# First stage of a hybrid block kernel: the order of the x, w_ada and w_in loads, and shift pieces summed on TensorE

## What is computed

```
sc = silu(c)
mod = sc @ w_ada + b_ada                       # w_ada: 1024 x 6144
sh1, sc1, ga1, sh2, sc2, ga2 = split(mod, 6)   # six chunks of 1024

h = rmsnorm(x, g_pre_mix) * (1.0 + sc1) + sh1
proj = h @ w_in                                # 1024 x 2560
uv = gelu(proj[..., :1024])                    # gMLP group
q, k, vv = split(proj[..., 1024:], 3)          # stick-breaking attention
...                                            # branches, w_out, residual with ga1
...                                            # second norm with sc2, sh2; router; 64 experts + shared; residual with ga2
```

## Time and profile before

| | us |
|---|---|
| runs shown: median | 1141.26 |
| lowest to highest of the 3 | 1138.83 to 1143.55 |
| the profiled execution | 1139.13 |
| its span, first to last instruction | 1137.4 |

### The profile page before, as it was taken

How to read it: one execution, slowest core, us unless ns; L and a number is a source line. 1 busy time by engine, 2 the same in 40 slices (tenths; PEclk the granted TensorE clock), 3 DMA queues, 4 the chain that set the end, 5 groups by cost and what they waited for, 6 DMA issues and landing times.

```text
span 1137.4 us, 14545 instructions
## 1 busy us (share of the span) xinstructions
PE 1042.1 (92%) x4500; PEld 725.2 (64%) x4500; DVE 761.9 (67%) x1282; ACT 568.2 (50%) x605; POOL 522.1 (46%) x222
## 2 busy tenths in 40 slices
PE   0699997979798999999999999999999999999975
PEld 0587775547663667766677667766677667666532
DVE  4649785652755677777777777777777777677247
ACT  4334135642341556655566556655566556655401
POOL 0233213540222466566655666566655666566300
PEclk9799998989998999999999999999999999999979
DMA  9756751202152599999999999999998889898296
GB/s 320 262 181 247 276 203 47 75 28 84 74 222 82 189 353 370 347 353 374 369 379 361 362 362 358 353 366 370 367 358 336 340 334 355 331 345 332 79 387 278
DMA packets 68903, 318.66 MB, mean 280 GB/s; under 512 B 18640, under 2 KB 19152, under 8 KB 41360
## 3 DMA queue, kind: packets, MB, share of 16 engines
q1 hardware_dynamic: 42096, 267.41, 61.4%
q0 software_dynamic: 23104, 47.50, 11.5%
q10 hardware_dynamic: 3680, 3.46, 1.0%
HBM read 317.25 MB, written 39.85 MB: 314 GB/s over the span
## 4 chain that ended last, share of the span: by engine, by line
PE 79%; DVE 9%; DMA 6%; issue 2%; ACT 2%; SPq 1%; ACTq 0%; DVEq 0%; POOLq 0%; POOL 0%
PE ps L1229 20%; PE ps L1210 11%; PE ps L1212 11%; PE ps L1211 11%; PE ps L942 8%; PE ps L993 7%; DMA yall<-y_rows 4%; PE ps L1143 2%; PE ps L1118 2%; DVE acc L1362 1%; DMA ada<-in_w_ada_dram 1%; PE ps L1049 1%; PE ps L1075 1%; PE ps L1163 1%; DMA hg<-h_rows,idxg 1%
## 5 line engine op out<-in xcount | busy, mean ns | idle before, releaser
L586 POOL DMA_INDIRECT hg<-h_rows,idxg x70 | 352.7, 5038 | 147.7 <-DVE idxg L1669 147.4
L1675 DVE TENSOR_TENSOR wlo<-raw,whi 128x2048 fp32r<-128x2048 f32 x134 | 300.6, 2285 | 0.0
L820 ACT ACTIVATE whi<-raw 128x2048 fp32r<-128x2048 f32 x136 | 261.4, 1923 | 0.1
L1229 PE MATMUL ps<-rawd,actt 128*128 128x512 f32 x544 | 244.5, 592 | 1.4 <-ACT actt L856 1.4
L1210 PE MATMUL ps<-whi,hthi 128*128 128x512 f32 x544 | 225.3, 414 | 0.0
L1212 PE MATMUL ps<-whi,htlo 128*128 128x512 f32 x544 | 213.0, 392 | 0.0
L1211 PE MATMUL ps<-wlo,hthi 128*128 128x512 f32 x544 | 212.8, 391 | 0.0
L1689 DVE TENSOR_TENSOR htlo<-ps,hthi 128x1024 fp32r<-128x1024 f32 x68 | 83.3, 1225 | 177.2 <-ACT hthi L852 177.2
L862 ACT ACTIVATE ysb<-ps 128x1024 f32<-128x1024 f32 x68 | 69.6, 1024 | 213.5 <-PE ps L1229 213.5
L1229 PEld LDWEIGHTS ps<-rawd,actt 128*128 128x128 f32 x544 | 102.8, 189 | 104.7 <-issue 97.8
L594 POOL DMA_INDIRECT y_rows<-ysb,idxs x68 | 73.2, 1076 | 161.1 <-ACT ysb L862 153.7
(11 more groups left out here) (247 smaller groups left out, 1283.0 us busy)
## 6 DMA issues: line engine op xcount, KB each, us to landing
raw<-in_w_gate_dram SPq DMA_DIRECT2D x68, 1024.0 KB, 7.6
raw<-in_w_up_dram SPq DMA_DIRECT2D x68, 1024.0 KB, 10.9
rawd<-in_w_down_dram SPq DMA_DIRECT2D x68, 1024.0 KB, 12.8
ada<-in_w_ada_dram SPq DMA_DIRECT2D x24, 1024.0 KB, 7.2
yall<-y_rows SPq DMA_DIRECT2D x8, 2048.0 KB, 24.3
wraw<-in_w_in_dram POOLq DMA_DIRECT2D x10, 1024.0 KB, 6.0
woraw<-in_w_out_dram SPq DMA_DIRECT2D x16, 256.0 KB, 2.7
xs<-in_x_dram SPq DMA_DIRECT2D x4, 512.0 KB, 10.8
```

The source lines that it names most:

```text
L586: gp.indirect_dma_start(out=hg[s][:, :, :].rearrange("p k q -> p (k q)"), out_offset=None, in_=h_rows, in_offset=bass.IndirectOffsetOnAxis ...
L820: A(whi[:, s, :, cols], raw[:, s, :, cols], ACT.Copy).then_inc(hi_ok, 1)
L1229: ins = mm(bank(4 + hf), actt[:, k, :], rawd[:, s, k, hf * 512:(hf + 1) * 512], start=(k == 0), stop=(k == KF - 1))
L1675: V.tensor_tensor(wlo[s][:, :, c0:c1], raw[:, s, :, c0:c1], whi[:, s, :, c0:c1].bitcast(F32), ALU.subtract).then_inc(lo_dve, 1)
```

## The change

Four things are moved, all in the first stage.

1. **SP's order.** x goes ahead of every piece of w_ada; then come the four SH1 pieces, the four SC1 pieces, then w_in pieces 0 and 1 (which POOL issued before), then GA1 and the rest. The ring `ada` has six buffers for the first eight pieces: pieces 0 to 5 go without a wait, 6 and 7 wait for `sh_mm` (PE is done with pieces 0 and 1). From piece 8 on there are two buffers.
2. **SH1 on PE.** For each SH1 piece PE runs four matmuls (two rows k, two halves of 512 columns) with sc_col[:, k] as the stationary operand (one column) and the piece as the moving one, adding up in banks 5 and 6, one partition. ACT copies the row of 1024 to `sh_row`, and eight matmuls with a strided set of 128 of its elements (one partition) as the stationary operand and a single one as the moving one bring it into columns. The transposes of z (k = 0 to 4) stand between the two, the others behind the scale's column sums.
3. **DVE** works out 1/rms first, then weighs only the four SC1 pieces.
4. **ACT and POOL.** `gb` and `bsp` are loaded by POOL instead of ACT and counted by `col_in`, for which DVE waits before a1c. `piece_high(0)` stands ahead of the wait for a1c and b1c, no longer behind k = 3.

The diff, cut to its core:

```diff
@@ sync @@
+            for t in range(TT):
+                sp.dma_start(xs[:, t, :], x[t * P:(t + 1) * P, :]).then_inc(x_in[t], 16)
...
+                if n == FIRST:
+                    load_win(0)
+                    load_win(1)
+                if ADA_SLOTS <= n < FIRST:
+                    sp.wait_ge(sh_mm, n - ADA_SLOTS + 1)
+                elif n >= FIRST:
+                    sp.wait_ge(ada_used, n - 5)
@@ gpsimd @@
+                gp.dma_start(gb[:, :], g_branch.rearrange("(k p) -> p k", p=P)).then_inc(col_in, 16)
+                gp.dma_start(bsp[:, :], b_spatial.rearrange("g i -> i g")).then_inc(col_in, 16)
@@ scalar @@
+            ac.wait_ge(sh_mm, 4)
+            A(sh_row[:, :], bank(5, 2)[0:1, :], ACT.Copy).then_inc(sh_ok, 1)
+            piece_high(0)
             ac.wait_ge(ab_ok, 1)
...
-                if k == KH - 1:
-                    piece_high(0)
@@ tensor @@
+            def shift_row(n):
...
+                pe.wait_ge(ada_in[ADA_SLOT[n]], 16 * ada_count(n))
+                for r in range(2):
+                    k = 2 * q + r
+                    for hf in range(2):
+                        ins = mm(bank(5 + hf)[0:1, :], sc_col[:, k:k + 1], ada[ADA_SLOT[n]][:, r, hf * 512:(hf + 1) * 512],
+                                 start=(k == 0), stop=(k == KD - 1))
+                ins.then_inc(sh_mm, 1)
@@ vector @@
+            factor(ST_X, D)
+            v.sem_inc(rs_x_ok, 1)
+            for n in range(FIRST // 2, FIRST):
                 weigh_piece(n)
...
+            v.wait_ge(vec_in, 16 * 4)
+            v.wait_ge(col_in, 16 * 2)
             v.wait_ge(mod_mm, 2)
```

More of the change, by code:

```diff
@@ L36 @@
 WO_RING = 3
+ADA_SLOTS = 6
 DG = 512
@@ L80, in block_kernel @@
         yall = at("yall", [P, TT, TOPK, D], F32, 0)
-        ada = [at("ada0", [P, 2, D], F32, 0), at("ada1", [P, 2, D], F32, 8 * KB),
-               at("ada2", [P, 2, D], F32, 136 * KB)]
+        ada = [at(f"ada{s}", [P, 2, D], F32, (0, 8, 136, 112, 120, 128)[s] * KB) for s in range(ADA_SLOTS)]
+        sh_row = at("sh_row", [1, D], F32, 188 * KB)
         acc = at("acc", [P, 2, D], F32, 16 * KB)
@@ L224, in block_kernel @@
         vec_in = sem("vec_in")
+        col_in = sem("col_in")
+        win_first = [sem(f"win_first{s}") for s in range(2)]
         row_in = sem("row_in")
         grow_in = sem("grow_in")
-        ada_in = [sem(f"ada_in{s}") for s in range(3)]
+        ada_in = [sem(f"ada_in{s}") for s in range(ADA_SLOTS)]
+        sh_mm = sem("sh_mm")
+        sh_ok = sem("sh_ok")
         ada_used = sem("ada_used")
@@ L348, in block_kernel, with ada_piece, ada_count @@
         SC1, SH1, GA1, SC2, SH2, GA2 = 1, 0, 2, 4, 3, 5
[L349 to L355, removed]
+        FIRST = 8
+        ADA_SLOT = [0, 1, 2, 3, 4, 5, 0, 1] + [n % 2 for n in range(FIRST, 24)]
+        def ada_piece(n):
+            return n // 4, n % 4
+        def ada_count(n):
+            return ADA_SLOT[:n + 1].count(ADA_SLOT[n])
+        CHUNKS = [SH1, SC1, GA1, SC2, SH2, GA2]
         COLG = [DG, 0, 2 * DG, 2 * DG + 512, 2 * DG + 1024]
@@ L405, in _, with load_win @@
             sp.dma_start(c_col[:, :], c.rearrange("(p k) -> p k", k=KD)).then_inc(c_in, 16)
-            for n in range(4 * len(CHUNKS)):
[L407 to L413, removed]
+            for t in range(TT):
+                sp.dma_start(xs[:, t, :], x[t * P:(t + 1) * P, :]).then_inc(x_in[t], 16)
+            def load_win(i):
+                g, h = i // 2, i % 2
+                sp.dma_start(wraw[:, i % 2], win_v[:, KH * h:KH * (h + 1), COLG[g]:COLG[g] + 512])\
+                  .then_inc(win_first[i], 16)
+            for n in range(4 * len(CHUNKS)):
+                g, q = ada_piece(n)
+                if n == FIRST:
[5 more added lines that the diff above has]
+                    sp.wait_ge(ada_used, n - 5)
                 if n == 16:
@@ L532, in _ @@
             gp.sem_inc(const_ok, 1)
[L535 to L542, removed]
+            with nc.allow_non_contiguous_dma(reason="two short vectors by column"):
+                gp.dma_start(gb[:, :], g_branch.rearrange("(k p) -> p k", p=P)).then_inc(col_in, 16)
+                gp.dma_start(bsp[:, :], b_spatial.rearrange("g i -> i g")).then_inc(col_in, 16)
+            for i in range(1, PIECES + 1):
+                if 2 <= i < PIECES:
+                    gp.wait_ge(wphi_ok, i - 1)
+                    gp.wait_ge(wplo_dve, i - 1)
+                    gp.wait_ge(wplo_pool, i - 1)
                     g, h = i // 2, i % 2
@@ L950, in h1_transposes @@
                 ins.then_inc(h1_tr, 1)
-            for k in range(KD - 1):
-                h1_transposes(k)
[L955 to L961, removed]
+            def shift_row(n):
+                _, q = ada_piece(n)
+                pe.wait_ge(ada_in[ADA_SLOT[n]], 16 * ada_count(n))
[5 more added lines that the diff above has]
+                ins.then_inc(sh_mm, 1)
+            pe.wait_ge(sc_ok, 1)
+            for n in range(FIRST // 2):
+                shift_row(n)
+            pe.wait_ge(z_ok, TT)
+            for k in range(5):
+                h1_transposes(k)
+            pe.wait_ge(sh_ok, 1)
+            shifts = sh_row[:, :].rearrange("p (q k) -> p k q", k=KD)
+            for k in range(KD):
+                ins = mm(ps[:, 7 * BANK + KD + k:7 * BANK + KD + k + 1], shifts[:, k, :], ones[0:1, 0:1],
+                         start=True, stop=True)
+            ins.then_inc(mod_mm, 1)
+            pe.wait_ge(acc_ok, 1)
+            cols = acc[:, 0, :].rearrange("p (q k) -> p k q", k=KD)
+            for k in range(KD):
+                ins = mm(ps[:, 7 * BANK + k:7 * BANK + k + 1], cols[:, k, :], ones[:, 0:1], start=True, stop=True)
+            ins.then_inc(mod_mm, 1)
+            for k in range(5, KD - 1):
+                h1_transposes(k)
             pe.wait_ge(h1_act, H1_BANK[KD - 1] + 1)
@@ L1014, in _ @@
             pe.wait_ge(h1_act, KD)
[L1015 removed]
+            pe.wait_ge(vec_in, 16 * 4)
             for g in range(GROUPS):
```

42 lines of the change are left out of this document (18 added, 24 removed).

## The result

The changed kernel takes **1131.2 us** (median of 6 runs, 1130.07 to 1132.02) against 1141.5 (6 runs): ratio 0.9912, 95% interval 0.9895 to 0.9929, so about 10 us less. A later set gave 0.9892 (0.987 to 0.9915). In the profiled execution the span went from 1137.4 to 1128.3.

A forecast was written before the change was run, and what follows sets the result against it. Transfers were taken to set the pace until 35 us, then PE's column sums and h1. Project(0) 6.2 us earlier (3.4 to the first h1 pass, 2.7 behind it) took 1141.3 to 1135.1 us, range 1131.5 to 1141.8.

The forecast's parts named there:

- Transfers: First-stage loads: 10.75 MB at 359 GB/s, last scale piece landing at 33.0 us, bounds 31.9 and 33.9.
- late landing of up to 2 us: First shift piece: landed at 11.5 us by the transfer rate, up to 2 us late, taken as 13.0.
- Shift rows: 16 matmuls on PE: 13.8 us at 2.4 GHz, 4.4 us of their time at 1.2 GHz, ending at 28.9.
- rival of a low clock throughout: PE's shift rows stay at the lower clock, take 27.5 us, and the kernel slows to 1147.7 us; chance 0.10.
- shift columns end at 34.7, hidden with 0.9 to spare: PE's eight column sums of the shift take 3.83 us and end before DVE's last weighing at 35.6.
- The first h1 pass before, 43.53: End of the modulation stage: first h1 pass at 40.1 instead of 43.5, a gain of 3.4 us.
- h1 to project(0): From first h1 pass to project(0): 6.6 us instead of 9.3, a gain of 2.7 us.
- the same clock cost: Projections: project(0) again charged 4.54 us at 1.2 GHz, within 1.5 us either way; no wait before project(1).
- the 6.2 of the forecast: Start of project(0): 46.7 instead of 52.86, 6.2 us earlier, carried through to the kernel's end.
- Later: Behind the projections: GA1's third piece, no longer fetched ahead, takes 7.2 us from about 67, hidden by some 5 us.
- Given back behind project(0): Rival, 77 to 116 us: a late piece or clock fall takes 2 to 4 us, 1137 to 1139; chance 0.10.

The follow-up runs named there:

- warm: The changed kernel with 44 transposes of the identity on PE ahead of the shift rows, nothing left out; 1132.26 us, one run.
- high_early: The kernel before, with ACT's rounding of w_in piece 0 moved ahead of the wait for a1c and b1c; ratio 0.997 (0.995 to 0.9991).
- high_mid: The changed kernel, with ACT's rounding of w_in piece 0 put back behind the fourth h1 pass; ratio 0.9924 (0.9898 to 0.995).
- pad_pe: The kernel before, with 16 one-column float32 matmuls at PE's head whose results are overwritten; ratio 0.9959 (0.9937 to 0.9982).

## Why the forecast was too small

- **Transfers: right at the end, by two errors that offset.** The last scale piece was put at 33.0 and landed at 32.9, DVE ended at 35.7 (35.6). But the first shift piece came at 15.1 instead of 13.0, beyond its late bound of 13.5: the "late landing of up to 2 us" was 3.6. The pieces behind it made up for it; they landed 2.6 us apart, not 2.9, since the queues then moved 408 to 420 GB/s and not 359.
- **Shift rows: the price right, the start and clock on the bad side.** 13.9 us warm (13.8), one stationary column does raise the clock, and the rival of a low clock throughout falls. The end was put at 28.9 (28.1 to 29.8) and came at 31.6 and 29.9.
- **The step that failed in the stage: "shift columns end at 34.7, hidden with 0.9 to spare".** They ended at 37.8 and 36.2. PE set the first h1 pass, at 42.5 and 40.8 instead of 40.1. One partition or 128 made no difference (3.96 and 3.97 us for eight sums, where 3.83 was charged). Here the trace agrees with the Trainium skill (TensorE: Matmul & The Clock Gate, LDWEIGHTS (loading the stationary operand)): the columns of the stationary operand count, not its partitions.
- **The first h1 pass before, 43.53, was an early one**: four more profiles lie at 43.9 to 44.6. Against the 43.53 the gain was 1.0 and 2.7; by the means it is 2.4, where 3.4 was forecast.
- **h1 to project(0): 6.6 forecast, 6.41 measured**, with the wait ended by DVE's `wplo` as said; 2.9 us instead of 2.7, shown in high_early and high_mid.
- **Projections: "the same clock cost" was 0.8 us too high** by the means (24.4 before, 23.6 after). That is one profile's doing: the clock was low for 2.1 us of project(0) in the first and for 4.4 in the second. So the gain up to the end of project(1) is 6.1 us (5.1 in the first two profiles): the 6.2 of the forecast, by terms that partly offset, and so partly by luck.
- **The step that failed in the sum: "Later", put at nothing.** By the profiles it holds 3.65 of the missing 4 us: 1.35 in ACT's row loads and 2.3 in the last read. The prediction asked whether GA1's load would come in time (it did) and not what its absence does to ACT's issues. It held the experts, and the read behind them, for untouched: their instructions are, the place of the code fetches among them is not. That term is not the worth of any step of the change; 16 idle matmuls give it to the old kernel too.
- **Given back behind project(0): fell.** No wait came in where the prediction looked for one.

What of the change pays is the order of the loads, the buffers and the early rounding. The rounding has runs of its own; the order and the six buffers no run takes apart. The shift rows on TensorE, its named core, pay nothing: without them the kernel is faster.

## What to carry to other kernels

An edit of a few dozen instructions can move later code fetches of that engine; before a change of some tenths of a per cent is credited with its gain, look whether a code packet has moved into or out of a bulk transfer, and repeat with padding. A step priced as "hidden with 0.9 us to spare" behind a start that is uncertain by 2 us is not hidden: give the spare the same bounds as the sum, and take the stage's times of before from several profiles. When an edit relieves one engine, check first that this engine was late; DVE kept pace with the transfers either way.

## What the runs showed of the hardware

- A 16 KB packet of code in a bulk read of 16.8 MB made it 2.3 us longer (43.8 to 44.5 against 41.7 to 41.9 us).
- The issue of one DMA on ACT took 0.45 to 0.95 us in the rows shown, and up to 1.46 in pad_pe, by what else was under way.
- Matmuls with a single stationary column and 512 moving ones raised the clock to 2.4 GHz, 2.8 or 5.05 us after they began in two executions of one program; 20.6 us of matmuls with one moving column did not. Transposes alone raised it after 5.0 us (warm).
- Two 4-byte-element loads that took 15.9 and 21.0 us on ACT's queue, behind other loads, took 6.7 and 6.8 on POOL's.
- A DVE product of 128x8 that took 0.17 us in thirteen profiles took 1.56 beside a POOL instruction that ended with it (high_early).
